# Two-layer hybrid decoder trunk, the stage before the layers: 22 transfers moved from SyncE's queue to ScalarE's, and the first modulation summed with 32x32 turns

## The reference, cut to what matters

```python
c_act = jax.nn.silu(c)
for l in range(DEPTH):
    mod = c_act @ ada_w[l] + ada_b[l]                  # 1024 x 6144 matrix, one row of c_act
    sh1, sc1, g1, sh2, sc2, g2 = split(mod, 6)
    h = rmsnorm(x, norm1_g[l]) * (1.0 + sc1) + sh1
    proj = h @ w_in[l]
    ...
```

## Time and profile before

| | |
|---|---|
| median of 3 runs | 2325.01 us (2323.96 to 2326.4) |
| the profiled execution, its own time | 2329.56 us |
| its span in the trace | 2327.1 us (2.46 us lie around it) |
| instructions | 30806 |
| TensorE busy (matmul) | 2264.4 us, 97% |
| VectorE busy | 1628.7 us, 70% |
| ScalarE busy | 1098.3 us, 47% |
| GpSimd busy | 1008.1 us, 43% |
| DMA | 311.08 MB in 273012 packets, mean 134 GB/s |
| start of the first layer's first instruction | 49.2 us after the start of the span |

### The profile page before, as it was taken

The page is one execution under the profiler, slowest core; times in us unless marked ns, Lnnn a source line. Parts: engine busy times, 40 slices in busy tenths (PEclk is TensorE's granted clock), DMA queues, the critical chain, the costliest instruction groups (busy, mean ns, idle before and its releaser), DMA issues.

```text
span 2327.1 us, 30806 instructions
## 1 busy us (share of the span) xinstructions
PE 2264.4 (97%) x11289; PEld 1833.2 (79%) x11289; DVE 1628.7 (70%) x2095; ACT 1098.3 (47%) x1808; POOL 1008.1 (43%) x641
## 2 busy tenths in 40 slices
PE   6999999999899999999999999999989999999998
PEld 5888866787788888888878787668878888888887
DVE  6885458449876666777888744672796767677886
ACT  4345546434444444444543464662444444444455
POOL 1222377444987777300012124043389777760000
PEclk7999999999999999999999999999999999999999
DMA  8742323342333333487557131004313333347763
GB/s 292 281 151 62 88 64 110 109 127 73 93 116 96 117 98 117 149 286 253 153 215 245 55 81 51 1 30 171 118 55 113 113 91 114 91 131 259 257 208 113
DMA packets 273012, 311.08 MB, mean 134 GB/s; under 512 B 37033, under 2 KB 191647, under 8 KB 271839
## 3 DMA queue, kind: packets, MB, share of 16 engines
q1 hardware_dynamic: 272174, 307.94, 40.7%
q10 hardware_dynamic: 688, 1.18, 0.2%
HBM read 246.53 MB, written 61.49 MB: 132 GB/s over the span
## 4 chain that ended last, share of the span: by engine, by line
PE 85%; DVE 7%; issue 2%; ACT 2%; POOL 1%; DMA 0%; DVEq 0%; SPq 0%; ACTq 0%; POOLq 0%
PE bank L1497 31%; PE bank L1067 18%; PE bank L1512 17%; PE bank L1127 6%; PE bank L1328 2%; PE bank L1360 1%; PE bank L1288 1%; DVE hLo L2150 1%; PE bank L1388 1%; DVE xT L2144 1%; PE bank L1217 1%; DVE xT L2472 1%; DVE tLo L2541 1%; ACT swaProb L1872 1%; PE bank L1195 1%
## 5 line engine op out<-in xcount | busy, mean ns | idle before, releaser
L987 POOL TENSOR_TENSOR wLo<-raw,wHi 128x1024 fp32r<-128x1024 f32 x66 | 161.5, 2448 | 411.4 <-ACT wHi L989 411.4
L1690 POOL TENSOR_TENSOR prodLo<-comb,prodHi 128x512 fp32r<-128x512 f32 x160 | 234.0, 1470 | 122.0 <-ACT prodHi L1029 122.0
L1497 PE MATMUL bank<-tHi,prodHi 128*128 128x512 f32 x640 | 249.9, 390 | 5.7 <-DVE tLo L2541 4.2
L1497 PE MATMUL bank<-tLo,prodHi 128*128 128x512 f32 x640 | 249.1, 389 | 0.0
L1497 PE MATMUL bank<-tHi,prodLo 128*128 128x512 f32 x640 | 249.1, 389 | 0.0
L1512 PE MATMUL bank<-gateHi,downHi 128*128 128x512 f32 x616 | 240.3, 390 | 0.0
L1512 PE MATMUL bank<-gateHi,downLo 128*128 128x512 f32 x616 | 239.7, 389 | 0.0
L1512 PE MATMUL bank<-gateLo,downHi 128*128 128x512 f32 x616 | 239.7, 389 | 0.0
L1029 ACT ACTIVATE prodHi<-comb 128x512 fp32r<-128x512 f32 x160 | 100.9, 634 | 249.0 <-PE bank L1497 228.7
L2486 DVE SCALAR_TENSOR_TENSOR ub<-bank,ffp,ub 128x1023 f32<-128x1023 f32 x88 | 112.8, 1282 | 141.9 <-ACT ub L1958 140.3
L1497 PE MATMUL bank<-hHi,prodHi 128*128 128x512 f32 x480 | 187.1, 390 | 7.1 <-POOL prodLo L1690 4.5
(11 more groups left out here) (393 smaller groups left out, 5346.4 us busy)
## 6 DMA issues: line engine op xcount, KB each, us to landing
raw<-in_ffn_w_up_dram SPq DMA_DIRECT2D x88, 512.0 KB, 4.8
gateRaw<-gateOut SPq DMA_DIRECT2D x154, 256.0 KB, 4.2
adaE<-in_ada_w_dram SPq DMA_DIRECT2D x64, 512.0 KB, 6.5
gateOut<-gateSums SPq DMA_DIRECT2D x22, 1024.0 KB, 5.5
raw<-in_w_in_dram SPq DMA_DIRECT2D x34, 512.0 KB, 4.1
downRaw<-in_ffn_w_down_dram SPq DMA_DIRECT2D x66, 256.0 KB, 3.8
raw<-in_w_out_dram SPq DMA_DIRECT2D x28, 512.0 KB, 3.8
downCols<-in_ffn_w_down_dram SPq DMA_DIRECT2D x24, 512.0 KB, 3.6
```

Of the source, the lines that this page charges most:

```text
L987: eng.tensor_tensor(lo[:], raw[slot][:], fview(hi[:]), ALU.subtract).then_inc(s["split_lo"], 1)
L1497: last = mm(o, w[idx][:, c0], moving(idx, kp, hi), start=kp == 0 and q_ == 0, stop=kp == 3 and q_ == 2)
L1690: pool.tensor_tensor(sLoW[idx][:], product_source(js, idx), fview(sHiW[idx][:]), ALU.subtract).then_inc(s["us_lo"], 1)
```

## The change

Two edits, both in the stage before the layers.

First, 22 of the transfers are issued by ScalarE at the start of its list: `posi`, the five pieces of the first two tiles of `w_in`, and the 16 of `load_params`. ScalarE's first computation (`cact`) comes after them in its list. SyncE keeps `crow`, `ropec`, the eight x tiles and the 16 `adaw` tiles, without anything between them.

Second, `adas[0]` and `adas[1]` are no longer summed over the partitions by 16 one-column matmuls. VectorE turns each in 32x32 blocks (into `nt[2]`), adds up groups of 32 (into `foldP`, 128x2x32), and TensorE finishes both parts with four matmuls against `quad` (`quadSum`, 128x32, already there). The bias is added while VectorE would otherwise go on, and the last additions become two instructions.

```diff
-                sp.dma_start(posi[64:128, :], positions.to_broadcast([64, T])).then_inc(s["small_loaded"], 16)
...
-                for i in range(8):
+                for i in range(2 * KT):
                     load_adaw(i)
-                load_params(sp, lambda w: w[0:1], prow)
-                for i in range(8, 2 * KT):
-                    load_adaw(i)
-                for n in range(AHEAD):
-                    load_win(sp, w_in[0:1], n, n, s[f"next_loaded{n}"])
...
-                pe.wait_ge(s["ada_done"], KT - 1)
-                part_sums(adas[0], 0, caus01[:, P - 1:P])
                 spread_rms(pe, "n1")
-                pe.wait_ge(s["ada_done"], 2 * KT - 2)
-                part_sums(adas[1], HALF, caus01[:, P - 1:P])
+                pe.wait_ge(s["ada_done"], 2 * KT)
+                for r in range(4):
+                    last = pe.matmul(bank[3][32 * r:32 * r + 32, 16:16 + 2 * KT], quad[:], foldP[:].rearrange("p j c -> p (j c)")[:, r:2 * 32:4],
+                                     start=True, stop=True)
+                last.then_inc(s["ada_sum"], 1)
...
             def _(act):
+                act.dma_start(posi[64:128, :], positions.to_broadcast([64, T])).then_inc(s["small_loaded"], 16)
+                for n in range(AHEAD):
+                    load_win(act, w_in[0:1], n, n, s[f"next_loaded{n}"])
+                load_params(act, lambda w: w[0:1], prow)
                 act.wait_ge(s["c_transposed"], 1)
...
+                    if k == KT - 1:
+                        if g:
+                            dve.wait_ge(s["ada_sum"], 2)
+                            dve.wait_ge(s["params_copied"], 1)
+                            link(dve.tensor_tensor(mod[:, 0:2 * KT], bank[3][:, 16 + 2 * KT:16 + 4 * KT], prm[:, R_ADAB:R_ADAB + 2 * KT], ALU.add))
+                        dve.wait_ge(s["ada_done"], KT * g + KT - 1)
+                        link(dve.transpose(nt[2][:], adas[g][:]))
+                        dve.tensor_reduce(foldP[:, g, :], nt[2][:].rearrange("p (c i) -> p c i", i=32), AX.X, ALU.add).then_inc(s["ada_done"], 1)
...
                 dve.wait_ge(s["ada_sum"], 3)
-                link(dve.tensor_copy(mod[:, 0:2 * KT], bank[3][:, 16 + 2 * KT:16 + 4 * KT]))
-                link(dve.tensor_tensor(mod[:, 0:KT], mod[:, 0:KT], bank[3][:, 16:16 + KT], ALU.add))
-                dve.wait_ge(s["ada_sum"], 4)
-                link(dve.tensor_tensor(mod[:, KT:2 * KT], mod[:, KT:2 * KT], bank[3][:, 16 + HALF:16 + HALF + KT], ALU.add))
-                first_modulation(dve)
+                link(dve.tensor_tensor(mod[:, 0:2 * KT], mod[:, 0:2 * KT], bank[3][:, 16:16 + 2 * KT], ALU.add))
+                dve.scalar_tensor_tensor(out=scl[:, 0, :], in0=mod[:, KT:2 * KT], scalar=1.0, in1=prm[:, R_N1:R_N1 + KT],
+                                         op0=ALU.add, op1=ALU.mult).then_inc(s["mod_first"], 1)
```

More of the change, by code:

```diff
@@ L466, in build @@
     adaw = [place(f"adaw{i}", [P, D], F32, at["h"] + 4 * K * i) for i in range(2 * KT)]
-    adas = [place(f"adas{g}", [P, D], F32, E[(12, 13, 15)[g]]) for g in range(3)]
+    adas = [place(f"adas{g}", [P, D], F32, E[12 + g]) for g in range(2)]
+    foldP = place("foldFirst", [P, 2, 32], F32, E[15])
     two_pi = 6.283185307179586
@@ L620, in _ @@
                 dve.wait_ge(s["c_act"], 1)
-                for n, i in enumerate([i for i in range(2 * KT) if i % KT]):
+                for i in [i for i in range(2 * KT) if i % KT]:
                     g, k = divmod(i, KT)
+                    n = i - 1
                     dve.wait_ge(s[f"ada_loaded{ADA_GROUP[i]}"], 16 * ADA_GROUP.count(ADA_GROUP[i]))
```

## The result

Slower. The changed kernel takes 2354.47 us (median of 4 runs, 2350.09 to 2363.41) against 2325.7 us before (4 runs, 2323.96 to 2329.17); the ratio is 1.0127, 95% interval 1.0094 to 1.0159. Timed once more beside other kernels it was 2353.69 us against 2326.46 us, ratio 1.0114 (1.0099 to 1.013). The forecast was 2352 us.

What follows compares the result with a forecast made beforehand. Bound: TensorE's chain behind the layer start at 49.23 us. ScalarE's first computation at 43.5 us plus 31.5 us ends the stage at 75.0 instead of 47.80: 2325.0 + 27 = 2352 us, range 2324.5 to 2355.

Steps and rivals of the forecast that it cites:

- Mechanism: Before the layers: queues alternate one 4 KB row with one short run, holding ScalarE's issues; +27 us, chance 0.48.
- VectorE's six tiles: Stage before the layers: six `adaw` tiles on VectorE behind the square root's reciprocal, taken from the old trace as 9.1 us.
- A pair of packets: On each transfer engine: one 4 KB row of SyncE's against one short run of ScalarE's, 0.173 us together.
- About 90 ahead: ScalarE's queue: a piece is accepted once about 90 runs an engine or fewer are ahead of it, bounds 80 and 150.
- From the issues to `cact`: ScalarE's start: parameters reached at 37.1 us, issued in 6.4 us, first computation at 43.5 us, 0.3 us for `cact`.
- To the square root: ScalarE before the layers: first copy of x to end of square root 18.4 us, with 0.3 us for `cact` before it.
- Part 1: Sums over the partitions at the stage's end: 3.7 us instead of 4.9 us, gain 1.2 us, bounds 0.5 and 2 us.
- Sum: End of the stage before the layers: ScalarE's first computation at 43.5 us plus 31.5 us, 75.0 us against 47.80 before.
- the likeliest case: Whole kernel: queues take turns packet by packet, +27 us, 2352 us, own range 2346 to 2355, chance 0.48.
- the parameters' possible hold: ScalarE's 16 parameter issues: if held as before the change, 9.4 us instead of 6.4, making the difference +30 us.
- By transfer: Rival on queue sharing: an engine serves one transfer's whole share, then the other queue's; +2.6 to +5.6 us, chance 0.28.
- as meant: Rival at ScalarE's start: short runs pass ahead of x or aren't held; +0.5 us, 2325.5 us, chance 0.20.

## Why the prediction came out as it did

**Mechanism: right.** Transfers pass packet by packet between two full queues, ScalarE is held at its issues, everything behind it moves, nothing else covers it. It was given 0.48, for no row of before could show the sharing. The Trainium skill (DMA: Bandwidth & Descriptors, Queues, rings and completion order) gives 9 to 17 descriptors as typical of a packet. These queues didn't pass in such blocks: 531 for 531, 949 for 949 with rows of half the length, and a short run at the end of each single row. What the page says of the round robin itself, by packet, agrees, with one row or run as the packet.

**The size: 27 us forecast, 26.3 to 28.8 measured, but with terms that cancel.** That they meet so closely is partly luck. The step that failed most is VectorE's six tiles, below. By the steps:
- *A pair of packets*: 0.173 us taken. From 7.52 to 33.41 us 171 an engine passed, 0.151 us each. The price of a row with its run was right: 9.95 MB in that stretch are some 2,430 rows, 0.171 us each on an engine. What I left out is that the packet by which each of SyncE's transfers ends (every ninth, as in 510 rows of 571 packets) lets a run pass too, and takes hardly any time. And until 7.52 they hadn't been one-for-one at all: 92 an engine through, where I had 25. Both made the hold end earlier.
- *About 90 ahead*: 54 to 97 measured; the hold went on into the parameters themselves (7.96 and 1.54 us). Together the last hold ended at 33.41 and not at 37.1, the issues at 38.66 and not at 43.5.
- *From the issues to `cact`*: the load of ScalarE's table, 1.28 us, stood at 0.80 before, hidden; behind the issues it isn't hidden. I had left it out. `cact` at 39.98: the 43.5 was 3.5 too late.
- *To the square root*: 18.5 us (39.98 to 58.45), 18.7 forecast.
- *VectorE's six tiles*: 12.9 us (58.48 to 71.37), 9.1 forecast. This step failed, by 3.8 us. I took the 9.1 from an execution in which GpSimd's low parts came behind the tiles (42.91); in the changed kernel ScalarE's high parts were made at once behind the root and the low parts ran beside the tiles. Kept apart, the last five take 6.84 us again instead of 10.72.
- *Part 1*: 71.28 to 74.79, 3.5 us, 3.7 forecast. Its gain, 1.2 us forecast, is 0.8 where it shows. The 4.9 us that I took as the old path seem to hold 0.64 us of waiting for GpSimd: the addition of the biases took 0.81 us and ended with GpSimd, where it takes 0.17 long after it.
- *Sum*: end at 74.79, 75.0 forecast.

**The range: its upper end, 2355, was too low.** The ratio 1.0127 on 2325.7 us gives 2355.2, just beyond, and single executions reach 2363.41. I had given the likeliest case 3 us above its value. That was the parameters' possible hold. It left out that engines which move together may meet (the 3.8 us of the six tiles), for which I had no term, and that executions of the changed kernel spread by 13 us. With the second measurement, 1.0114, the value lies at 2352.2; the two intervals overlap.

**The rivals.** *By transfer* (+3.5) and *as meant* (+0.5) are excluded by the counts and by ScalarE's held issues. That ScalarE has free time from 5.9 to 10.19 us was true, and the run with `w_in` back at SyncE's end shows what it is good for: 17 issues that aren't held.

## What to carry to other kernels

In these runs an issue was free only while its queue took it. Before a list of transfers is put in front of an engine's work, count its runs, not its bytes or its issues (here some 54 to 97 an engine were taken ahead), and look at what the other queue holds, since each short run here waited for a whole long row. Put transfers of short runs on a queue whose engine nobody waits for, or behind the work that others wait for: the same five pieces cost 27 us in front and nothing measurable behind. And a chain that is moved brings its engines together anew: durations from the old trace hold only for the neighbours they had there.

## What the runs showed of the hardware that was not expected

- ScalarE's short runs had more than their turn until about 7 us (1,470 packets beside 443), and exactly their turn afterwards. Not explained here.
- VectorE's instruction with two inputs and GpSimd's subtraction aren't slowed evenly beside each other, they take turns. In the changed kernel's timeline:

```profile
59.97 2.87 POOL L446 TENSOR_TENSOR wLo<-raw,wHi 128x1024 fp32r<-128x1024 f32 x1 [56.39 <-ACT wHi L449]
...
60.65 3.27 DVE L629 SCALAR_TENSOR_TENSOR adas<-adaw,cact,adas 128x1024 f32<-128x1024 f32 x1
...
62.80 3.32 POOL L446 TENSOR_TENSOR wLo<-raw,wHi 128x1024 fp32r<-128x1024 f32 x1
...
64.03 3.18 DVE L629 SCALAR_TENSOR_TENSOR adas<-adaw,cact,adas 128x1024 f32<-128x1024 f32 x1
```

The tile that starts at 60.65 ends at 63.92, 1.1 us after the low part at 62.84, where alone it takes 1.28 (L628 before); the second low part ends 2.2 us after that, and the next tile 1.1 us after it. Each seems to wait for the other's end. The Trainium skill (SBUF — State Buffer, Who interferes with whom) has a pair of ports shared by the two as an exclusive lock, and a VectorE instruction with two inputs in SBUF contends for it with a GpSimd instruction that reads SBUF. These rows agree, and so do 6.84 and 4.64 us when they are kept apart.
